# Where the independent projections stand among the attention jobs of two latent sections

## The chip, the cores and the metric

The kernel runs on one core of one Trainium2 chip. The metric is the device time of one execution in microseconds. Engines are named as in the profile: PE is TensorE (PEld is its weight load), DVE is VectorE, ACT is ScalarE, POOL is GpSimd, SP issues the DMAs.

## The reference, cut to what matters

The model is two blocks of two layers each on 256 tokens of width 1024, all in float32. The change lies in the second block alone. One of its layers computes, for the 256 latent tokens and the 256 context tokens:

```
h  = x  * (1 + scale) + shift                       # scale, shift, gate from silu(c) @ w_ada
hc = cx * (1 + scale_c) + shift_c
(a_q, a_i, a_ff, a_fb, b_q.., c_q.., d_q.., g) = split(h @ w_in)     # 1024 x 3840, the same for hc
y_a = hgrn2 scan over a_*                # forget gates, in powers of two: 1, 2, 4, ... 128 tokens
y_b = global attention (b_*)             # keys and values of latent and context tokens, normed and rotated
y_c = differential attention (c_*)
y_d = windowed attention with a sink (d_*)
y   = concat(y_a, y_b, y_c, y_d) * silu(g)
x   = layer_norm(alpha * x + gate * (y @ w_out))
```

The first layer also carries the context tokens on to the second (`cx_new`); the second layer returns the latent tokens only.

## The kernel before

The program is five sections in a row: a prologue, `one0` and `one1` (the layers of the first block), `two0` and `two1` (the latent part of the second block's layers; most of the context's work lies in `one1`). Each section has a script, a flat list of items written by `script_two0` (L338 and on) and the like. Every engine walks the same script in the same order and issues only its own part of each item. So the script fixes the order on PE, ACT, DVE and POOL at once: an instruction that waits holds up all later items on its engine.

The items that matter here:

- A **unit** is an item with 1 MB of weights of its own, streamed by SP into a ring of five slots. `("proj", name, i, (q,))` projects 256 output columns of the latent (q = 0) or context tokens (q = 1); `("out", i, (1,))` does the same for the context's output. Either is 32 matmuls, 16 for each half (L1015, L1024, L1232), into one of three PSUM banks. `("half", unit)` in a script is the first 16 matmuls, the unit's own item the other 16. ACT (L1454, L1457) or DVE (L2121) drains the bank. A unit's event e may not start before bank e - 3 is drained.
- A **job** is an attention piece over 1024 logits columns: `logits` (PE L1100), a maximum on DVE (L1872, or L1880 with a mask, then L1895), the exponentials on ACT (L1493), `soft` (DVE: L1912, L1928), `turn` (eight or four transposes on PE, L1119, copied to SBUF by ACT, L1509) and `mix` (PE L1156, copied by DVE, L1954). There is one logits buffer: `logits` of job n waits until the exponentials of job n - 1 are done (`exps_done`). `mix` of a job waits for the ACT copy of its `turn`. Each latent section has 16 jobs: 0 to 3 global (G), 4 to 7 windowed (N), 8 to 15 differential (F).
- `level` (two events, 16 matmuls, L1259, merged by DVE L2205 to L2209) and `prep` (gaps on POOL L2321 to L2327, exponentials ACT L1549, products DVE L2190 and L2192) are the steps of the scan; `hout` closes it. `decay` is DVE L2158 and L2165 with ACT L1543; `gap` is DVE L2146 and L2150.
- `sq` and `norm` are a head norm: ACT squares (L1531), PE sums (L1241), ACT L1536 and L1538, DVE L2134. `rot` is the rotary embedding: DVE L1854 and L1858, POOL L2347 and L2355. `mean` and `var` (PE L1327 to L1340) are the layer norm of the context, `feed` (DVE L2019, ACT L1588) the context's input to the second layer, and `silu`, `gate`, `mod` are elementwise.

`weave` (L133) lays a section's list `fill` of 2 x 16 slots around the jobs. Slot 2n - 1 stands beside `logits` n, behind `level` and `mix` n - 2 and ahead of `soft` n; slot 2n stands behind `turn` n - 1. So PE meets, for n from 2: `logits n, level, mix n-2, slot 2n-1, turn n-1, slot 2n, logits n+1`.

`lay(fill, start, stop, items)` fills the slots: each unit becomes two pieces, its first half and its second half, an item without weights goes with the piece before it, and the pieces are spread evenly over the slots. In `two0` 14 units go into slots 1 to 23, in `two1` 11 units into slots 0 to 18. The scan's items are placed apart by `lay_scan`, the items of later slots by hand.

Of the kernel before, what the change touches and what calls it, by code (L numbers as in the profile page):

```python
# [85 lines left out]
def jobs_latent(layer):  # L86

    out = [Job(kind, qt, [(b, 0), (b, 1)], 2 * T, 0, layer) for kind in ("G", "N") for qt in (0, 1) for b in (0, 1)]
    return out + [Job("F", qt, [(h // 2, 2 * (h % 2)), (h // 2, 2 * (h % 2) + 1)], 2 * T, 0, layer)
                  for qt in (0, 1) for h in range(4)]  # L90
# [15 lines left out]
def has_unit(item):  # L106

    return item[0] in UNIT_KINDS
# [24 lines left out]
def weave(jobs, fill):  # L133


    s = []

    def more():
        return fill.pop(0) if fill else []

    for n in range(jobs + 2):
        items = []
        if n < jobs:
            items = more()
            s.append(("logits", n))
            s += beside(items, ("level",))
        if n >= 2:
            s.append(("mix", n - 2))
        s += beside(items, ("hout",)) + [i for i in items if i[0] not in ("level", "hout")]
        if n < jobs:  # L150
            s.append(("soft", n))
        if 1 <= n <= jobs:
            s.append(("turn", n - 1))
            s += more()
    return s


def group(tag, g):

    return [("mva", 2 * g, tag), ("mva", 2 * g + 1, tag)]  # L160
# [38 lines left out]
def proj(name, q=0, i=0):  # L199

    return ("proj", name, i, (q,))
# [51 lines left out]
def latent_scan():  # L253

    out = [[("prep", 0, 0)]]
    out += [([("level", 0, LEVELS[i - 1])] if i else []) + [("prep", 0, m)] for i, m in enumerate(LEVELS[1:])]
    return out + [[("level", 0, LEVELS[-2]), ("prep", 0, "qc")], [("level", 0, LEVELS[-1])], [("hout", 0)], [("sq", "h0")],
                  [("norm", "h0")]]
# [50 lines left out]
def lay(fill, start, stop, items):  # L309


    pieces = []
    for item in items:
        if isinstance(item, list):
            pieces[-1] += item
        elif has_unit(item):
            pieces += [[("half", item)], [item]]
        else:
            pieces[-1].append(item)
    for n, piece in enumerate(pieces):  # L320
        slot = fill[start + n * (stop - start) // len(pieces)]
        if piece[0][0] == "half" or ("half", piece[0]) in slot:
            slot += piece
        else:
            slot[0:0] = piece


def lay_scan(fill, start, steps):


    for n, items in enumerate(steps):
        fill[max(start + 2 * (n - 2), 0) if n < 12 else start + n + 6] += items


def script_two0():

    out = lambda i: ("out", i, (1,))
    s = [proj("kk"), proj("vv"), ("silu", 1), ("gate", 1, 0), ("gate", 1, 1), ("rot", "nk", 0), ("sq", "gk0"), proj("gq"), ("norm", "gk0"),  # L338
         ("sq", "gq0"), proj("ff"), proj("fb"), ("rot", "gk", 0), ("gap", 0), ("norm", "gq0"), ("half", out(0)), ("rot", "gq", 0),
         ("decay", 0), out(0)]  # L340
    jobs = jobs_latent(0)
    fill = [[] for _ in range(2 * len(jobs))]
    fill[0] += [proj("hq")]
    lay_scan(fill, 3, latent_scan())
    fill[24] += [("silu", 0), ("gate", 0, 0)]
    for h, items in ((22, [("gap", 1)]), (23, [("decay", 1)]), (25, [("prep", 1, "khat")]), (27, [("khatT", 1)]), (29, [("state", 1)])):
        fill[h] += items
    lay(fill, 1, 24, [proj("nq"), out(1), ("rot", "nq", 0), out(2), out(3), proj("fk"), ("mean", 1),
                      proj("fq"), ("var", 1), ("rot", "fk", 0), ("mod", "v1"), proj("fv"), ("rot", "fq", 0), proj("hi"), ("feed", 1, "v1"), proj("ff", 1),
                      proj("fb", 1), proj("g"), proj("g", 0, 1), proj("g", 0, 2), proj("g", 0, 3)])  # L350
    lay(fill, 25, 32, [proj("hi", 1)] + [("outa", i, (0,)) for i in range(3)])
    s += weave(len(jobs), fill)
    s += [("sq", "f0"), ("half", ("outa", 3, (0,))), ("norm", "f0"), ("outa", 3, (0,)), ("gate", 0, 1), proj("vv", 1), ("outb", (0,))]
    return s + [("mean", 0), ("half", proj("kk", 1)), ("var", 0), ("feed", 0, "v1"), proj("kk", 1)]


def script_two1():

    s = [proj("kk"), ("sq", "gk1"), proj("vv"), ("norm", "gk1"), ("rot", "nk", 0), ("sq", "gk0"), proj("gq"), ("norm", "gk0"),
         ("sq", "gq0"), proj("ff"), ("affine", 0, 0), proj("fb"), ("rot", "gk", 0), ("gap", 0), ("norm", "gq0"), ("half", proj("hq")), ("rot", "gq", 0),  # L360
         ("decay", 0), proj("hq")]
    jobs = jobs_latent(1)
    fill = [[] for _ in range(2 * len(jobs))]
    lay_scan(fill, 1, latent_scan())
    fill[15] += [("silu", 0)]
    fill[20] += [("gate", 0, 0)]
    lay(fill, 0, 19, [proj("nq"), proj("g"), ("rot", "nq", 0), proj("g", 0, 1), proj("fk", 1), proj("fk"), proj("g", 0, 2), ("rot", "fk", 0),
                      proj("fq"), proj("g", 0, 3), ("rot", "fq", 0), proj("hi"), proj("fv"), proj("fv", 1)])
    for g, h in ((4, 19), (5, 21)):
        fill[h] += group("v1", g)  # L370
        fill[h + 1].append(("row", g))
    for i in range(4):
        fill[22 + i].append(("flip", i))
    lay(fill, 24, 32, [("outa", i, (0,)) for i in range(3)])
    n = next(h for h, items in enumerate(fill) if ("norm", "h0") in items)
    fill[n].remove(("norm", "h0"))
    fill[n].insert(0, ("norm", "h0"))
    s += weave(len(jobs), fill) + [("sq", "f0"), ("half", ("outa", 3, (0,))), ("norm", "f0"), ("gate", 0, 1), ("outa", 3, (0,))]
    return s + [("outb", (0,)), ("settle", 0), ("settle", 1)]
# [105 lines left out]
for _args in (("prologue", PROLOGUE, 1), ("one0", script_one0(), 1, 0, JOBS_ONE),  # L485
              ("one1", script_one1(), 1, 0, JOBS_ONE + jobs_ctx()),
              ("two0", script_two0(), 2, 0, jobs_latent(0)), ("two1", script_two1(), 2, 1, jobs_latent(1))):
    SECTIONS.append(Section(*_args, before=SECTIONS[-1] if SECTIONS else None))
# [1983 lines left out]
```

## Time and profile before

| | |
|---|---|
| Time, median of 3 runs | 1391.55 us (1390.64 to 1391.55) |
| The profiled execution | 1388.96 us, span 1387.2 us |
| PE busy | 1339.2 us (97%) |
| PEld busy | 1114.7 us (80%) |
| DVE, ACT, POOL busy | 51%, 31%, 12% |
| Mean granted TensorE clock | 0.992 of full |
| DMA | 224.89 MB, mean 162 GB/s |

Busy PE is not PE at its peak: matmuls are pipelined, and their ends are modelled. The bracket at the end of a timeline line is the idle time of the engine ahead of it, and the instruction that ended it; "xN" is how many instructions of one line and shape follow one another. In the profile `two0`'s job 0 begins at 923.3 us and `two1`'s at 1201.1 us.

### The profile page before, as it was taken

To read this page: it belongs to the slowest core of one execution; us is meant where nothing else is said; L and a number is where in the kernel's file an instruction comes from. 1 tells how busy PE (TensorE), PEld (TensorE's weight loads), DVE (VectorE), ACT (ScalarE), POOL (GpSimd) and SP (SyncE) were. 2 spreads that over 40 slices of the span, in tenths; PEclk is the share of its full clock that TensorE was granted. 3 is DMA by queue.
4 is the path that set the end of the run, shared out by engine and by line. 5 is a ranking of instruction groups with operands and counts; after the bars stand their busy time and mean duration, and the time that the engine had idled before them with its cause. 6 is when DMAs were issued, how large, how long until landed. Compare 5 with 4: busy or idle time off the path is not lost.

```text
span 1387.2 us, 18957 instructions
## 1 busy us (share of the span) xinstructions
PE 1339.2 (97%) x7394; PEld 1114.7 (80%) x7394; DVE 704.8 (51%) x1525; ACT 423.5 (31%) x776; POOL 168.2 (12%) x191
## 2 busy tenths in 40 slices
PE   6999999999899999989999999999999999999996
PEld 4888888888788888868888888887788788888864
DVE  1449677556223868414234442256674632656566
ACT  2322222311121222244323222342353513533442
POOL 0302200000020120000111100032220000323000
PEclk9999999999999999999999999999999999999999
DMA  9647557668434645534333343442222333522330
GB/s 383 271 165 285 190 192 260 222 239 316 173 127 147 242 180 185 198 119 145 129 121 122 124 143 103 148 151 92 92 91 92 116 143 122 198 92 94 111 130 31
DMA packets 31913, 224.89 MB, mean 162 GB/s; under 512 B 3920, under 2 KB 4048, under 8 KB 5072
## 3 DMA queue, kind: packets, MB, share of 16 engines
q1 hardware_dynamic: 31824, 223.68, 44.6%
q8 instruction: 59, 0.97, 0.3%
q14 instruction: 30, 0.25, 0.1%
HBM read 222.62 MB, written 1.05 MB: 161 GB/s over the span
## 4 chain that ended last, share of the span: by engine, by line
PE 87%; DVE 4%; issue 3%; DMA 2%; ACT 2%; SPq 1%; POOL 0%; DVEq 0%; ACTq 0%; POOLq 0%
PE event L1024 45%; PE event L1015 11%; PE event L1168 6%; PE event L1232 5%; PE logits L1100 4%; PE mixed_out L1156 3%; PE turns L1119 2%; DMA region<-in_quick 2%; PE event L1259 2%; PE event L1198 2%; PE event L1193 2%; PE turns L990 1%; PE logits L990 1%; PE turns L1114 1%; PE logits L1114 1%
## 5 line engine op out<-in xcount | busy, mean ns | idle before, releaser
L1024 PE MATMUL event<-u,ring 128*128 128x256 f32 x3072 | 683.7, 381 | 2.9 <-ACT u L1397 2.4
L1024 PEld LDWEIGHTS event<-u,ring 128*128 128x128 f32 x3072 | 578.6, 190 | 92.4 <-issue 15.8
L1015 PE MATMUL event<-ring,u 128*128 128x256 f32 (+1 forms) x704 | 151.1, 372 | 0.0
L1015 PEld LDWEIGHTS event<-ring,u 128*128 128x128 f32 x704 | 127.4, 190 | 18.5 <-issue 3.0
L2347 POOL TENSOR_TENSOR raw<-raw,tables 128x512 f32<-128x512 f32 (+1 forms) x28 | 44.5, 1591 | 695.0 <-DVE turned L1854 513.8
L1457 ACT ACTIVATE region<-event 128x512 f32<-128x512 f32 x72 | 43.0, 597 | 280.2 <-PE event L1024 280.0
L1493 ACT ACTIVATE S<-logits,stat 128x512 f32<-128x512 f32 (+2 forms) x160 | 83.9, 536 | 129.3 <-DVE stat L1895 124.9
L1781 DVE CUSTOM_DVE_ANT_0 region<-ring,u 128x1024 f32<-128x1024 f32 x80 | 103.8, 1298 | 2.8
L1232 PE MATMUL event<-region,ring 128*128 128x256 f32 x384 | 86.7, 385 | 2.3 <-DVE x L2121 2.3
L1168 PE MATMUL event<-region,ring 128*128 128x256 f32 x384 | 84.4, 380 | 0.1
L1232 PEld LDWEIGHTS event<-region,ring 128*128 128x128 f32 x384 | 73.5, 193 | 13.7 <-issue 3.7
L1168 PEld LDWEIGHTS event<-region,ring 128*128 128x128 f32 x384 | 72.6, 190 | 11.2 <-issue 0.9
L1100 PE MATMUL logits<-region 64*128 64x256 f32 (+4 forms) x320 | 60.9, 483 | 8.9 <-DVE region L2134 6.1
L1872 DVE TENSOR_REDUCE stat<-logits 128x2 f32<-128x1024 f32 (+1 forms) x32 | 39.2, 1224 | 59.2 <-PE logits L1100 58.7
L1509 ACT ACTIVATE PT<-turns 128x1024 f32<-128x1024 f32 (+1 forms) x52 | 44.7, 860 | 55.2 <-PE turns L1119 54.5
L1156 PE MATMUL mixed_out<-PT,region 128*64 128x128 f32 (+2 forms) x584 | 55.6, 300 | 1.7 <-ACT PT L1509 1.7
L1156 PEld LDWEIGHTS mixed_out<-PT,region 128*64 128x64 f32 x584 | 39.0, 139 | 19.0 <-issue 11.1
L2190 DVE TENSOR_TENSOR region<-region 128x512 f32<-128x512 f32 x24 | 19.1, 797 | 57.8 <-ACT region L1549 31.2
L1880 DVE CUSTOM_DVE_ANT_0 logits<-logits,tables 128x128 f32<-128x128 f32 (+2 forms) x48 | 22.9, 477 | 50.1 <-PE logits L1100 45.6
L2209 DVE COPY_PREDICATED region<-tables,event 128x512 f32<-128x512 uint32 x42 | 30.8, 734 | 34.3 <-PE event L1259 32.9
L1100 PEld LDWEIGHTS logits<-region 64*128 64x128 f32 (+1 forms) x320 | 24.8, 188 | 28.4 <-issue 23.2
L2321 POOL TENSOR_TENSOR region<-region 128x256 f32<-128x256 f32 x24 | 17.0, 708 | 248.6 <-PE event L1259 145.3
(257 smaller groups left out, 1360.9 us busy)
## 6 DMA issues: line engine op xcount, KB each, us to landing
ring<-in_w SPq DMA_DIRECT2D x196, 1024.0 KB, 4.9
region<-in_quick SPq DMA_DIRECT2D x8, 1024.0 KB, 18.2
region<-in_rows SPq DMA_DIRECT2D x1, 1536.0 KB, 8.1
tables<-in_two SPq DMA_DIRECT2D x1, 1472.0 KB, 8.0
x<-in_x SPq DMA_DIRECT2D x1, 1024.0 KB, 5.9
u<-in_cond_rows SPq DMA_DIRECT2D x1, 1024.0 KB, 7.9
x<-in_ctx SPq DMA_DIRECT2D x1, 1024.0 KB, 6.7
out<-x SPq DMA_DIRECT2D x4, 256.0 KB, 2.2
```

What stands on the lines that cost most here:

```text
L1015: ins = mm(bank[:, t * 256:t * 256 + width], mem.u[:, q, k, t * P:(t + 1) * P], wt[:, k * 256:k * 256 + width], start=k == 0, stop=k == KB ...
L1024: ins = mm(bank[:, j * 256:(j + 1) * 256], wt[:, k * 256 + j * P:k * 256 + j * P + P], mem.u[:, q, k, :], start=k == 0, stop=k == KB - 1)
L1100: ins = mm(out, q, k, start=True, stop=True)
L1156: ins = mm(out, value_of(mem, job, m, kt), turned[:, :, kt, :], start=kt == 0, stop=kt == tiles - 1)
L1168: ins = mm(bank[:, j * 256:(j + 1) * 256], wt[:, at:at + P], mem.one["y"][:, 4 * br + k, :], start=k == 0, stop=k == 3)
L1232: ins = mm(bank[:, j * 256:(j + 1) * 256], wt[:, at:at + P], src[:, k, :], start=k == 0, stop=k == KB - 1)
L1457: act(dst, split2(bank), func, scale=scale).then_inc(drained[e % BANKS], 1)
L1493: ins = act(S[:, m * K:(m + 1) * K], mem.LG[:, m * K:(m + 1) * K], ACT.Exp, bias=stat[:, 1, m:m + 1], accum_out=stat[:, 2, m:m + 1])
L1509: act(mem.PT[:, n % 2, 0:cols], mem.TR[:, 0:cols], ACT.Copy).then_inc(sems["turns_copied"], 1)
L1781: ins = eng.tensor_tensor_reduce(out=mem.scratch, in0=part, in1=times, scale=1.0, scalar=0.0, op0=ALU.mult, op1=ALU.add, accum_out=mem.mod ...
L1872: eng.tensor_reduce(stat[:, 0, 0:nm], mem.LG[:, 0:nm * K].rearrange("p (m k) -> p m k", m=nm), AX.X, ALU.max).then_inc(mine, 1)
L2347: tt(shape(mem.raw), shape(mem.raw), wide(cosine, width // T), ALU.mult).then_inc(mine, 1)
```

## The change

`lay` is replaced by `lay_whole(fill, first, last, items)` for the main filling of both sections; slots, jobs, the scan's items and everything behind job 12 are as before, and no instruction is added or dropped.

```
+def lay_whole(fill, first, last, items):
+    units = []
+    for item in items:
+        if has_unit(item):
+            units.append([item])
+        else:
+            units[-1].append(item)
+    jobs = last - first + 1
+    for k in range(jobs):
+        own = units[k * len(units) // jobs:(k + 1) * len(units) // jobs]
+        n = 2 * (first + k) - 1
+        if len(own) == 1:
+            fill[n] += [("half", own[0][0])]
+            fill[n + 1][0:0] = own[0]
+        else:
+            for i, unit in enumerate(own):
+                if 2 * i < len(own):
+                    fill[n] += unit
+                else:
+                    fill[n + 1][0:0] = unit
 ...
-    lay(fill, 1, 24, [proj("nq"), out(1), ("rot", "nq", 0), out(2), out(3), proj("fk"), ("mean", 1),
+    lay_whole(fill, 1, 11, [proj("nq"), out(1), ("rot", "nq", 0), out(2), out(3), proj("fk"), ("mean", 1),
 ...
-    lay(fill, 0, 19, [proj("nq"), proj("g"), ("rot", "nq", 0), proj("g", 0, 1), proj("fk", 1), proj("fk"), proj("g", 0, 2), ("rot", "fk", 0),
+    lay_whole(fill, 1, 9, [proj("nq"), proj("g"), ("rot", "nq", 0), proj("g", 0, 1), proj("fk", 1), proj("fk"), proj("g", 0, 2), ("rot", "fk", 0),
```

A job with one unit has its first half beside `logits` and its second behind the next `turn`; a job with two has one whole unit in each place. Read on PE, the scripts go from the left column to the right one (context units have a '; "/2" is a second half, "1/2" a first half; `level`, `mix`, `prep` are left out; "|" is the `turn`):

| `two0`, after logits | before | after |
|---|---|---|
| 1 | 1/2 nq, nq/2 \| 1/2 out1 | 1/2 nq \| nq/2 |
| 2 | out1/2, rot nq \| 1/2 out2 | 1/2 out1 \| out1/2, rot nq |
| 3 | out2/2, 1/2 out3 \| out3/2 | 1/2 out2 \| out2/2 |
| 4 | 1/2 fk \| fk/2, mean | out3 \| fk, mean |
| 5 | 1/2 fq \| fq/2, var, rot fk, mod, 1/2 fv | 1/2 fq \| fq/2, var, rot fk, mod |
| 6 | fv/2, rot fq \| 1/2 hi | 1/2 fv \| fv/2, rot fq |
| 7 | hi/2, feed \| ff' | 1/2 hi \| hi/2, feed |
| 8 | 1/2 fb' \| fb'/2 | ff' \| fb' |
| 9 | 1/2 g \| g/2 | 1/2 g \| g/2 |
| 10 | g1 \| 1/2 g2 | 1/2 g1 \| g1/2 |
| 11 | hout, g2/2, sq h \| norm h, gap', 1/2 g3 | hout, sq h, g2 \| g3, norm h, gap' |
| 12 | g3/2, decay' \| silu, gate | decay' \| silu, gate |

| `two1`, after logits | before | after |
|---|---|---|
| 0 | nq | nothing |
| 1 | 1/2 g \| g/2, rot nq | 1/2 nq \| nq/2 |
| 2 | 1/2 g1 \| g1/2 | 1/2 g \| g/2, rot nq |
| 3 | 1/2 fk' \| fk'/2, 1/2 fk | 1/2 g1 \| g1/2 |
| 4 | fk/2 \| 1/2 g2 | 1/2 fk' \| fk'/2 |
| 5 | g2/2, rot fk \| 1/2 fq | fk \| g2, rot fk |
| 6 | fq/2 \| g3, rot fq | 1/2 fq \| fq/2 |
| 7 | 1/2 hi \| hi/2 | 1/2 g3 \| g3/2, rot fq |
| 8 | silu, 1/2 fv \| fv/2 | silu, 1/2 hi \| hi/2 |
| 9 | 1/2 fv' \| fv'/2 | fv \| fv' |

## Rows read from the trace of the kernel before

**Rows 1.** The page, section 1: busy us, share of the span, instructions.

```profile
PE 1339.2 (97%) x7394; PEld 1114.7 (80%) x7394; DVE 704.8 (51%) x1525; ACT 423.5 (31%) x776; POOL 168.2 (12%) x191
```

**Rows 2.** Timeline of `two0`'s first jobs: start us, us, engine, line, operation, [idle before].

```profile
924.35 7.17 PE L1024 MATMUL event<-u,ring 128*128 128x256 f32 x32
931.46 1.13 PE L1100 MATMUL logits<-region 64*128 64x512 f32 x4
...
939.53 1.04 PE L1119 MATMUL turns<-consts,S 128*128 128x128 f32 x8
940.40 3.62 PE L1232 MATMUL event<-region,ring 128*128 128x256 f32 x16
943.95 1.13 PE L1100 MATMUL logits<-region 64*128 64x512 f32 x4
...
951.77 3.69 PE L1232 MATMUL event<-region,ring 128*128 128x256 f32 x16 [0.26 <-DVE x L2121]
...
964.18 5.38 PE L1232 MATMUL event<-region,ring 128*128 128x256 f32 x16 [2.09 <-DVE x L2121]
969.39 1.04 PE L1119 MATMUL turns<-consts,S 128*128 128x128 f32 x8
```

**Rows 3.** Windows: busy us of each engine, then granted clock, DMA share, GB/s.

```profile
964.50:967.90 3.40, 3.40 (x10) 2.68 (x9) 3.10 (x8) 0.00 (x0) 0.00 (x0) 0.50 0.54 224
602.00:609.50 7.50, 3.60 (x24) 2.84 (x24) 2.13 (x3) 2.85 (x4) 0.00 (x0) 0.55 0.16 66
```

**Rows 4.** Timeline of PE: two stalls elsewhere.

```profile
605.90 2.08 PE L1100 MATMUL logits<-region 64*128 64x256 f32 x8 [6.07 <-DVE region L2134]
...
999.57 1.10 PE L1335 MATMUL event<-u,consts 128*128 128x256 f32 x4 [2.48 <-DVE u L1363]
1000.51 3.62 PE L1015 MATMUL event<-ring,u 128*128 128x256 f32 x16
```

**Rows 5.** Timeline of `two0`, jobs 7 to 13: feed, head norm, turn.

```profile
1023.29 7.14 PE L1024 MATMUL event<-u,ring 128*128 128x256 f32 x32 [0.51 <-ACT u L1588]
...
1077.24 1.12 PE L1241 MATMUL event<-rs,consts 128*128 128x512 f32 x2 [0.97 <-ACT rs L1531]
...
1079.91 0.75 DVE L2134 SCALAR_TENSOR_TENSOR region<-region,par,rs 128x512 f32<-128x512 f32 x1 [7.46 <-ACT rs L1538]
...
1083.30 1.22 DVE L1872 TENSOR_REDUCE stat<-logits 128x2 f32<-128x1024 f32 x1
...
1086.09 0.20 ACT L1493 ACTIVATION_READ_ACCUMULATOR S<-logits,stat 128x1 f32 x1
...
1087.91 1.13 PE L1100 MATMUL logits<-region 32*128 32x512 f32 x4
1088.27 1.06 ACT L1543 ACTIVATE region<-region 128x1024 f32<-128x1024 f32 x1
1089.36 0.60 ACT L1509 ACTIVATE PT<-turns 128x512 f32<-128x512 f32 x1
...
1090.01 1.09 PE L1156 MATMUL mixed_out<-PT,region 128*64 128x128 f32 x8 [0.97 <-ACT PT L1509]
```

**Rows 6.** Timeline of `two1`'s job 0.

```profile
1201.07 1.13 PE L1100 MATMUL logits<-region 64*128 64x512 f32 x4 [0.61 <-POOL region L2355]
...
1203.84 1.23 DVE L1872 TENSOR_REDUCE stat<-logits 128x2 f32<-128x1024 f32 x1
...
1206.62 0.20 ACT L1493 ACTIVATION_READ_ACCUMULATOR S<-logits,stat 128x1 f32 x1
```

**Rows 7.** Timeline of `two1`, jobs 6 to 8.

```profile
1278.10 0.72 DVE L1854 STREAM_SHUFFLE turned<-raw 128x512 f32<-128x512 f32 x1
...
1280.75 1.26 POOL L2355 TENSOR_TENSOR region<-raw,turned 128x512 f32<-128x512 f32 x1
1281.42 1.13 PE L1100 MATMUL logits<-region 64*128 64x512 f32 x4
...
1290.23 0.88 DVE L1928 TENSOR_SCALAR S<-S,stat 128x512 f32<-128x512 f32 x2
1292.37 1.13 PE L1100 MATMUL logits<-region 32*128 32x512 f32 x4
```

**Rows 8.** The page, section 6: issues of the ring, KB each, us to landing.

```profile
ring<-in_w SPq DMA_DIRECT2D x196, 1024.0 KB, 4.9
```

## The prediction

> **What bounds the kernel now.** I read the page's busy times first: PE is busy for 1339.2 of 1387.2 us [rows 1], so it sets the end nearly everywhere, and the change adds and drops no instruction. It can act in two ways only: by PE's stalls, taken away or added, and by the clock that follows a stall. The second view is therefore the timeline of PE alone over both latent sections, where a bracket behind a row is a stall; the third is the timeline of all engines around each stall and around each place where the new order has less work on PE; the fourth, windows, for the granted clock.
>
> The reader is to see three things. First, PE's work comes in fixed bricks. A whole unit runs from 924.35 to the logits at 931.46, 7.11 us; a half from 940.40 to 943.95, 3.55 us [rows 2]. Twice a half is a whole, so cutting a unit costs nothing by itself. A job adds logits (1.0), level (1.0), mix (1.0 with sixteen matmuls) and turn (0.9): about 11 us with a unit. Second, stalls are few: 0.26, 2.09 [rows 2], 2.48 [rows 4], 0.51, 0.97 and 0.97 us [rows 5] in `two0`, and none above 0.2 us in `two1` from its first logits up to job 10. Third, behind the stall of 2.09 us the granted clock is 0.50 for 3.4 us [rows 3], its lower level, 1.2 instead of 2.4 GHz: the half that starts at 964.18 lasts until 969.39, 5.21 us in place of 3.55 [rows 2]. The stall so cost another 1.66 us behind it. Behind 6.07 us of stall in `one1` the clock is low again: 0.55 over 7.5 us, with 3.6 us of PE's work in them [rows 3, 4]. Behind 2.48 us it is not: the half at 1000.51 takes 3.62 us [rows 4]. So a stall above 2 us may bring the low clock, a long one does.
>
> **What goes.** In `two0`, `1/2 out2` and `1/2 out3` started right behind the unit before, and waited for DVE to drain a bank (0.26 and 2.09 us). Now `logits`, `level` and `mix`, 3.0 us of PE, lie between a unit and the next, more than the longer of the two waits. Gain 0.26 + 2.09 + 1.66 = 4.01 us [rows 2]. `ff'` used to begin right behind `hi/2` and waited 0.51 us for the feed; now logits, level and mix come first, while the feed keeps its distance from `hi/2`. Gain 0.51 us [rows 5]. The head norm's sum waited 0.97 us for `sq h`, with one half and a turn as cover; now g2 and g3 whole, 14 us, cover it. Gain 0.97 us [rows 5]. The wait of `mix 11` (0.97) is taken into the new sum below. The wait for `var` (2.48 us) stays: between `mean` and `var` the order is the same to the item. Sum of gains: 4.01 + 0.51 + 0.97 + 0.97 = 6.46, say 6.5 us.
>
> **What comes, A: job 12 of `two0`.** The wait for the exponentials of job 12 is the one to watch. Behind the head norm's sum stand, on DVE, the norm's product (starts 2.67 us after the sum, at 1079.91), then `gap'`, and only then the maximum of logits 12, at 1083.30; the exponentials end at 1086.29. That is 1086.29 - 1077.24 = 9.05 us from the sum, and PE's own position did not set it, since logits 12 was done before DVE came free [rows 5]. PE used to fill these 9 us with two halves of g3; both now lie ahead of the sum. Left are the sum (1.0), logits 12 (1.1), mix 10 (1.0, eight matmuls) and turn 11 (0.5): 3.6 us. Logits 13 waits 9.05 + 0.1 - 3.6 = 5.6 us. Behind it on PE are mix 11 and hi'; mix 11 also needs ACT's copy of turn 11, which stands behind the exponentials and the logarithm of `decay'`: 1.06 + 0.60 = 1.7 us [rows 5], against 1.1 us of logits 13, another 0.6 us. A = 6.2 us. Lower bound: 3.6, if `gap'` (1083.30 - 1080.66 = 2.6 us of DVE) ran ahead of the product, which DVE's order forbids; upper: 7.2, if ACT still had a drain of g3 to do in between, as it had before.
>
> **B: job 0 of `two1`.** Before, nq (7.1 us) stood between logits 0 and logits 1. Now nothing does: PE's next work needs the exponentials of job 0. DVE comes to the maximum only after the scans of `decay`, at 1203.84, and ACT ends at 1206.82 [rows 6]. Logits 0 ends its slot at 1202.1, so PE stands for 1206.82 + 0.1 - 1202.1 = 4.8 us. Queued behind logits 1 are level 0, 1/2 nq and turn 0; turn 0 then comes later than its probabilities, so no second stall. I see no bound below 4: nothing on DVE or ACT comes sooner through this change.
>
> **C: logits 8 of `two1`.** `rot fq` moves from a place ahead of logits 7 to one right ahead of logits 8, the first logits that need it. Job 7 itself keeps its order on PE (logits, level, mix, half, turn, half: 1281.42 to 1292.37). On DVE `rot` now follows soft 7, which ends at 1290.23 + 0.88 = 1291.11; the rotation takes from 1278.10 to 1282.01, 3.91 us over DVE and POOL [rows 7]. Hence 1295.0, against logits 8 at 1292.37: with 0.1 for the signal a stall of 2.7 us. Bounds: 0, if soft 7 comes 2.7 us sooner, to 5.4, twice the value, if POOL still runs gaps of the scan when the rotation reaches it. Behind logits 8 wait level, mix 6 and 1/2 hi.
>
> **The clock.** A and B are near the 6.07 us stall, so the lower level is expected behind both: 3.4 us of work at half speed, 1.7 us each; of A's, 0.5 us is work under which the 0.6 us wait of mix 11 disappears. C is near the stalls of 2.09 and 2.48 us, one with and one without: 0.6 x 1.7 = 1.0 us. Together 1.2 + 1.7 + 1.0 = 3.9 us; bounds 0 and 3 x 3.4 = 10.
>
> **What costs nothing.** Ring: the units keep their order, SP asks for the next as one ends, a load lands in 4.9 us [rows 8] while five slots hold 35 us of work; two whole units in a row do not change that. If the cover were gone, one load would cost up to 4.9. DVE in the windowed jobs: soft 7 ends 9.7 us after its logits (1281.42 to 1291.11) in a job of 10.95 us; `rot nq` and `rot fk`, 1.4 us of DVE, now stand at the end of jobs 2 and 5 with one more job before their reader. DVE's next maximum can be late by up to 1.5 us, but PE asks for its result only 11 us later. I take 0; bound 3.
>
> Cuts: in `two0` 8 units are cut by other items instead of 11, in `two1` 7 instead of 9. Rows 2 price a cut at nothing. The Trainium skill (TensorE: Matmul & The Clock Gate, "Step-by-step: what each phase is for") has PE pull a weight load ahead of running matmuls only where row groups do not conflict or a background buffer takes it; by that rule a switch between the 64-row matmuls of level and the full-height ones could leave a load in the open. At the mean load of 1114.7 / 7394 = 0.15 us [rows 1] five cuts fewer would be worth 0.8 us of gain. The row shows none of it.
>
> **Sum.** 6.2 + 4.8 + 2.7 + 3.9 - 6.5 = +11.1 us, on the profiled execution's 1388.96: 1400.1 us. The median of the runs is 2.6 us above that execution; the forecast goes on the median: 1391.55 + 11.1 = 1402.6 us.
>
> **Rivals.**
>
> 1. *Faster.* Bank turnaround is what counts. A unit that is open across `level` leaves no spare bank, and its successor waits for DVE; once cured, the pace of the whole section rises and A, B and C find DVE early. It would give at least -6.5 us, 1385 us; it decides once A + B + C with their clock stay under 6.5 us. For it: the 2.09 us row and its clock [rows 2, 3]. Against it: A and B are read off chains on DVE and ACT that do not wait for PE. The Trainium skill's rule (Trainium Kernel Development and Optimization, "Performance Expectations") that weight-load share and not matmul share tells the distance from the bound speaks for this case: 80% against 97% [rows 1]. But in an unbroken unit a matmul takes 7.11 / 32 = 0.22 us with a load beside it, so much of that room is not idle time. Chance 0.03.
> 2. *The clock stays up* behind the new stalls: +7.2 us, 1398.7. For it: the 2.48 us stall. Against it: both long ones are above 4 us. Chance 0.20.
> 3. *DVE falls behind* in jobs 3 to 7, where the rotations now come between a softmax and the next maximum: two more stalls of about 1.5 us and one more fall of the clock, +4.7 on top, 1407.3. For it: the 2.09 us stall was one by DVE [rows 2]. Against it: the credit of one job. Chance 0.17.
> 4. *Nothing to measure*: only B is real, A and C are hidden: 4.8 + 1.7 - 6.5 = 0, 1391.6. Chance 0.04.
>
> The forecast itself has 0.56. The range, 1396 to 1408, holds cases 2 and 3 with it: its low end is +4.5 us, the sum with no fall of the clock and C hidden. A measurement of this kernel tells about 0.2%, 2.8 us, from no change: slower beyond that 0.93, within it 0.04, faster beyond it 0.03.
>
> **What would show it.** A: a stall of 5 to 6 us on PE ahead of logits 13 in `two0`, ended by ACT's exponentials. B: 4 to 5 us ahead of logits 1 in `two1`, by the same. C: 2 to 3 us ahead of the first differential logits of `two1`, ended by POOL's last addition (L2355). The clock at 0.5 for some 3.4 us behind A and B. No stall by L2121 between jobs 1 and 4 of `two0`, `mean` 4 us closer to job 0, no wait at `ff'` and at the head norm. It would be wrong if logits 1 or 13 started without a wait, or if new waits for banks or for DVE's products stood between jobs 1 and 10.

## The result and the profile after

The changed kernel takes 1403.24 us (median of 4 runs, 1400.79 to 1404.21), the kernel before 1391.37: a ratio of 1.0084, 95% interval 1.0072 to 1.0096, or +11.9 us. Forecast were 1402.6 us, a range of 1396 to 1408, and 0.93 for slower.

The page after has as many instructions on every engine but for two records of ACT, a little more busy time on PE, and a longer span:

```profile
span 1402.5 us, 18955 instructions
...
PE 1345.3 (96%) x7394; PEld 1119.6 (80%) x7394; DVE 699.6 (50%) x1525; ACT 420.9 (30%) x774; POOL 166.8 (12%) x191
```

Lines of the code have moved down by 24 (L1100 is L1124). The timeline of PE after, from the first logits of `two0`, at the places that answer to [rows 2, 4, 5]:

```profile
927.27 1.13 PE L1124 MATMUL logits<-region 64*128 64x512 f32 x4 [0.62 <-POOL region L2379]
...
958.40 3.72 PE L1256 MATMUL event<-region,ring 128*128 128x256 f32 x16
961.96 1.04 PE L1143 MATMUL turns<-consts,S 128*128 128x128 f32 x8
962.84 3.62 PE L1256 MATMUL event<-region,ring 128*128 128x256 f32 x16
966.38 1.13 PE L1124 MATMUL logits<-region 64*128 64x512 f32 x4
...
969.36 7.17 PE L1256 MATMUL event<-region,ring 128*128 128x256 f32 x32
976.37 1.04 PE L1143 MATMUL turns<-consts,S 128*128 128x128 f32 x8
...
984.15 0.59 PE L1351 MATMUL event<-u,consts 128*128 128x256 f32 x2
...
999.04 1.66 PE L1359 MATMUL event<-u,consts 128*128 128x256 f32 x4 [2.48 <-DVE u L1387]
1000.63 2.08 PE L1124 MATMUL logits<-region 64*128 64x512 f32 x4
...
1083.18 1.02 PE L1265 MATMUL event<-rs,consts 128*128 128x512 f32 x2
1084.13 1.13 PE L1124 MATMUL logits<-region 32*128 32x512 f32 x4
...
1086.20 0.66 PE L1143 MATMUL turns<-consts,S 128*128 128x128 f32 x4
1092.17 2.08 PE L1124 MATMUL logits<-region 32*128 32x512 f32 x4 [5.31 <-ACT S L1517]
...
1096.08 8.32 PE L1039 MATMUL event<-ring,u 128*128 128x256 f32 x32
1104.23 0.60 PE L1143 MATMUL turns<-consts,S 128*128 128x128 f32 x4
```

The first half of the list is what was hoped for: the out units start with no bracket behind them, and from the first logits to `mean` it takes 984.15 - 927.27 = 56.9 us, where it took 61.4 (984.67 - 923.29). Then come two losses. The wait for `var` is as long as before, 2.48 us, but now the clock falls behind it: `var`'s four matmuls take until the logits 1.59 us (999.04 to 1000.63) in place of 0.94 (999.57 to 1000.51 [rows 4]), and logits 6 takes 2.08 us in place of 1.13. And logits 13 stands still for 5.31 us (A).

The timeline of all engines between the norm's sum and logits 13, against [rows 5]:

```profile
1085.75 0.75 DVE L2158 SCALAR_TENSOR_TENSOR region<-region,par,rs 128x512 f32<-128x512 f32 x1 [16.59 <-ACT rs L1562]
...
1089.12 1.22 DVE L1896 TENSOR_REDUCE stat<-logits 128x2 f32<-128x1024 f32 x1
...
1091.92 0.20 ACT L1517 ACTIVATION_READ_ACCUMULATOR S<-logits,stat 128x1 f32 x1
```

From the sum to the end of the exponentials: 1092.12 - 1083.18 = 8.94 us, against 9.05 before. The chain on DVE and ACT is unchanged; what is gone is PE's work beside it.

In `two1`, against [rows 6, 7], PE:

```profile
1207.28 1.13 PE L1124 MATMUL logits<-region 64*128 64x512 f32 x4 [0.62 <-POOL region L2379]
1213.09 2.08 PE L1124 MATMUL logits<-region 64*128 64x512 f32 x4 [4.68 <-ACT S L1517]
...
1220.88 1.04 PE L1143 MATMUL turns<-consts,S 128*128 128x128 f32 x8
...
1300.73 1.13 PE L1124 MATMUL logits<-region 32*128 32x512 f32 x4 [2.73 <-issue]
```

and DVE and POOL ahead of the last of these:

```profile
1295.80 0.88 DVE L1952 TENSOR_SCALAR S<-S,stat 128x512 f32<-128x512 f32 x2
1296.73 0.01 DVE L1878 LOAD_MASK_SELECT turned<-raw  x1
1296.73 0.72 DVE L1878 STREAM_SHUFFLE turned<-raw 128x512 f32<-128x512 f32 x1
...
1299.37 1.26 POOL L2379 TENSOR_TENSOR region<-raw,turned 128x512 f32<-128x512 f32 x1
```

B is 4.68 us, ended by ACT. C is 2.73 us; the view puts it down to "issue", but POOL's last addition of the rotation ends at 1300.63, 0.1 us before logits 8 starts. Windows behind the four stalls (granted clock is the third number from the end), answering to [rows 3]:

```profile
999.00:1003.00 4.00, 3.96 (x14) 2.20 (x16) 3.83 (x6) 0.89 (x2) 3.00 (x2) 0.57 0.46 193
1092.00:1096.00 4.00, 3.83 (x12) 2.07 (x12) 2.63 (x6) 3.91 (x6) 0.04 (x1) 0.50 0.00 0
1213.00:1216.00 3.00, 2.91 (x14) 1.88 (x16) 1.38 (x3) 1.09 (x2) 2.69 (x5) 0.50 0.00 0
1300.70:1304.00 3.30, 3.27 (x37) 2.25 (x37) 1.96 (x3) 0.49 (x1) 0.00 (x0) 1.00 0.46 191
```

The clock fell behind `var`, A and B, not behind C. At `var` it fell about half a microsecond after its first matmul had started:

```profile
999.25:999.50 0.25, 0.25 (x2) 0.22 (x2) 0.25 (x1) 0.00 (x0) 0.00 (x0) 0.89 0.93 393
999.50:999.75 0.25, 0.25 (x2) 0.17 (x2) 0.22 (x2) 0.00 (x0) 0.00 (x0) 0.50 1.08 459
```

The kernel before kept the full clock over the same stretch:

```profile
999.50:1003.50 4.00, 3.93 (x18) 3.52 (x19) 3.83 (x6) 0.89 (x2) 3.01 (x2) 1.00 0.46 193
```

The account of the two profiled executions (1388.96 and 1404.21 us, 15.2 apart): 4.0 us lie ahead of `two0`'s first logits, in code that did not change (923.29 against 927.27); over the 14 profiled executions of this document this start lies between 923.29 and 928.21 us, so the 4.0 are scatter. `two0` went from 277.8 to 280.0 us (first logits to first logits of `two1`), +2.2; `two1` from 186.1 to 195.2 us (to the end of the span), +9.1. In `two1`, from logits 0 to turn 0 after, 13.60 us hold 6.6 us of bricks, so B costs 7.0: 4.7 of stall, 2.3 of low clock. With C's 2.7 that is 9.8, less 0.7 of small waits and cuts gone. In `two0`, from the norm's sum to turn 12, 21.05 us hold 12.65 us of bricks: A costs 8.4, of which 5.3 are stall and 3.1 low clock. The low clock behind `var` adds 1.7. Against these 10.1 stand 4.5 us up to `mean`, 0.5 of the feed, 1.9 of the two waits of 0.97, and 1.0 of smaller terms, which the account of the gains below names.

### The profile page after: what moved, and what is told of

Its sections match the earlier page's. It is cut to its first block, busy times and chain, and to the rows that moved or that the text cites. A ratio compares the mean times of both kernels' runs of the same rounds, so it can differ in the third digit from the quotient of the medians.

```text
span 1402.5 us, 18955 instructions
## 1 busy us (share of the span) xinstructions
PE 1345.3 (96%) x7394; PEld 1119.6 (80%) x7394; DVE 699.6 (50%) x1525; ACT 420.9 (30%) x774; POOL 166.8 (12%) x191
## 4 chain that ended last, share of the span: by engine, by line
PE 90%; DVE 5%; issue 3%; ACT 2%; DMA 1%; POOL 0%; SPq 0%; DVEq 0%; ACTq 0%; POOLq 0%
PE event L1048 44%; PE event L1039 11%; PE event L1192 6%; PE event L1256 5%; PE logits L1124 4%; PE mixed_out L1180 3%; PE turns L1143 3%; PE event L1283 2%; PE event L1222 2%; PE event L1217 2%; PE logits L1014 1%; PE turns L1014 1%; PE event L990 1%; PE event L1027 1%; ACT S L1517 1%
## 5 line engine op out<-in xcount | busy, mean ns | idle before, releaser
L1124 PE MATMUL logits<-region 64*128 64x256 f32 (+4 forms) x320 | 63.8, 501 | 21.7 <-ACT S L1517 11.4
L1124 PEld LDWEIGHTS logits<-region 64*128 64x128 f32 (+1 forms) x320 | 25.4, 193 | 42.4 <-issue 26.2
L1180 PEld LDWEIGHTS mixed_out<-PT,region 128*64 128x64 f32 x584 | 39.7, 140 | 18.7 <-issue 11.9
L1143 PE MATMUL turns<-consts,S 128*128 128x128 f32 x336 | 45.7, 274 | 0.0
```

What stands on the lines that cost most here:

```text
L1124: ins = mm(out, q, k, start=True, stop=True)
L1143: ins = eng.transpose(mem.TR[:, i * P:(i + 1) * P], S[:, at:at + P], c["ident"])
L1180: ins = mm(out, value_of(mem, job, m, kt), turned[:, :, kt, :], start=kt == 0, stop=kt == tiles - 1)
```

## The experiments

Theory: three covers were taken from PE (A, B, C), each a stall of known length, and a low clock behind some. Rivals: whole units cost by themselves; the low clock is hidden; the stalls are only moved. Each kernel was timed in 5 rounds beside the kernel before, whose median was 1391.3 to 1391.5 us in each of the three sets. "Under" and "over" are differences of medians against the changed kernel's 1403.24 unless something else is named. A ratio's interval is about 0.1% wide on each side, 1.5 us, so a difference of two changed kernels is good to about 2 us.

**The new filling in one section alone.**

```
 t0_only: script_two1 keeps  lay(fill, 0, 19, ...)
 t1_only: script_two0 keeps  lay(fill, 1, 24, ...)
```

> The new filling in two0 alone; two1 filled as before. Theory (the three stalls A, B, C and the clock behind them): two0 carries the gains of 6.5 us and A with its clock, 7.4 to 8.5 us, so +1 to +2.5 us against the kernel before, 1392.4 to 1394; no stall ahead of logits 1 and 8 of two1. Rival (whole units cost by themselves, spread over both sections): half of the 11.9 us, about +6 us, 1397.

> The new filling in two1 alone; two0 filled as before. Theory: B 4.7 us of stall with 2.4 us of clock, C 2.7 us, clock behind C 0 to 1.7 us: +9 to +10.5 us against the kernel before, 1400.4 to 1402. Rival (spread over both sections): about +6 us, 1397.

Measured: 1395.15 us, ratio to before 1.0027 (1.0018 to 1.0037), and 1400.92, 1.0068 (1.0056 to 1.0080). `two1` carries most, +9.6, as the three stalls have it. `two0` is +3.8, above the 1 to 2.5 expected: a miss. Its ten runs lie far apart, 1392.76 to 1398.36 us. The profile of one at 1396.73 shows the expected stalls and no others, but low clock behind `var` and also behind a stall of 2.07 us late in `two1` that all kernels have, and that the change does not touch:

```profile
1336.93 1.78 PE L1200 MATMUL event<-strips,consts 128*128 128x512 f32 x2 [2.07 <-DVE strips L1793]
```

(1.78 us for what takes 1.13 in the kernel before.) The spread over both sections that the rival wanted is refused.

**One cover given back at a time.**

```
 undo_a, script_two0:
+    fill[22].remove(proj("g", 0, 3))
+    fill[23].insert(0, proj("g", 0, 3))
 undo_b, script_two1:
+    fill[0] += [proj("nq")]
-    lay_whole(fill, 1, 9, [proj("nq"), proj("g"), ...
+    lay_whole(fill, 1, 9, [proj("g"), ...
 undo_c, script_two1:
+    fill[14].remove(("rot", "fq", 0))
+    fill[12].append(("rot", "fq", 0))
```

> The changed kernel with the unit g3 of two0 moved from ahead of the head norm's sum to behind mix 10 of job 12. Theory: logits 13 finds its exponentials done; the 5.3 us of stall and about 3 us of low clock go, a wait of under 1 us for the copy of turn 11 comes back: 7 to 8 us under the changed kernel, 1395.5 to 1396.5. Rival (the changed order of the head norm or the banks, not the missing cover, is what costs): under 2 us gained, above 1401.

> The changed kernel with nq of two1 put back whole behind logits 0, the other ten units over jobs 1 to 9. Theory: the 4.7 us of stall ahead of logits 1 go and 2.4 us of low clock: 7 us under the changed kernel, 1396. If the low clock behind a stall costs nothing, since later waits take it up, 4.7 us: 1398.5. Rival (DVE's pace in jobs 1 to 4 sets the time, the stall is only moved): no gain, 1403.

> The changed kernel with rot fq of two1 moved ahead of logits 7, behind fq. Theory: the 2.7 us of stall ahead of logits 8 go, and with them what the clock cost behind it, 0 in the profiled execution: 2.7 to 4 us under the changed kernel, 1399.2 to 1400.5. Rival (the profile puts this stall down to issue, not to POOL, so the order is not what ends it): no gain, 1403.

undo_a: 1395.25 us, 8.0 under. undo_b: 1396.84, 6.4 under. Both are near what was expected. (Two of the six runs of undo_a are at 1399 to 1400 us, the others at 1395; its profile, of a run at 1398.97, has low clock behind the stall C.) The timeline of PE of undo_a at the place of A: the long bracket is gone, and the 0.97 us of [rows 5] is back.

```profile
1085.77 1.13 PE L1126 MATMUL logits<-region 32*128 32x512 f32 x4
1087.86 1.09 PE L1182 MATMUL mixed_out<-PT,region 128*64 128x128 f32 x8 [0.97 <-ACT PT L1535]
```

undo_c: 1403.05 us, 0.2 under: nothing, where 2.7 to 4 were expected. Yet the stall itself did go. The timeline of PE of undo_c at logits 8, and 45 us later at the stall of 2.07 us:

```profile
1295.43 3.62 PE L1050 MATMUL event<-u,ring 128*128 128x256 f32 x16
1298.98 1.13 PE L1126 MATMUL logits<-region 32*128 32x512 f32 x4
...
1344.31 1.16 PE L1202 MATMUL event<-strips,consts 128*128 128x512 f32 x2 [2.07 <-DVE strips L1795]
...
1346.25 2.07 PE L1126 MATMUL logits<-region 32*128 32x512 f32 x4
1348.25 1.97 PE L1182 MATMUL mixed_out<-PT,region 128*64 128x128 f32 x8
```

Logits and mix take twice their time. From that stall's end to the first `outb` matmul it is 1386.92 - 1344.31 = 42.6 us, after the change 1385.47 - 1346.07 = 39.4: 3.2 us of low clock, which paid back C. The mean granted clock that is on record for every timed run points the same way: 0.982 to 0.984 in the five runs of undo_c, 0.985 to 0.986 in the four of the changed kernel. The next experiment puts it to the test.

**The stall behind it filled.** Four matmuls that nobody reads, 1.8 us of PE, in the 2.07 us stall of the changed kernel, of undo_c and of the kernel with all three moves:

```
             elif kind == "row":
+                if item[1] == 5:
+                    eng.wait_ge(drained[e % BANKS], w.fills(e - BANKS))
+                    for _ in range(4):
+                        mm(mem.bank[e % BANKS][:, 0:256], c["ident"], mem.consts[:, 0:256], start=True, stop=True)
```

> The changed kernel with 4 filler matmuls (1.8 us of PE) in the 2.07 us stall ahead of the last mva transposes of two1 (row 5). Theory: this stall is followed by low clock in some executions and not in others, worth up to 3.2 us: 0 to 2 us under the changed kernel, 1401.2 to 1403.2.

> The kernel with rot fq moved ahead of logits 7, with the same 4 filler matmuls. Theory: the 2.7 us that this move took out of PE came back as low clock behind the later stall of 2.07 us (3.2 us in the profiled execution); with that stall filled the move shows: 2.7 to 3.2 us under the kernel without the filler, 1400, and 1.5 to 3 us under the changed kernel with the filler. Rival (the move itself gives nothing): no difference to the changed kernel with the filler.

Measured: 1402.50 and 1399.73. With the later stall filled, the move of `rot fq` is worth 2.8 us, its stall; the ranges, 1402.07 to 1403.58 and 1398.86 to 1402.24, just touch. On the changed kernel the filler does 0.7, within the uncertainty, and there the profile had shown no low clock at this place. So the 2.7 us of C are very likely real, and in undo_c they came back as low clock 45 us later.

**All three moves, without and with the filler.**

> All three moves together: g3 of two0 behind mix 10 of job 12, nq of two1 behind logits 0, rot fq ahead of logits 7. Theory: 7.5 + 7 + 2.7 = 17.2 us under the changed kernel, 1386, which is 5.4 us under the kernel before: whole units are then as good as halves or better. Rival (the gains overlap, or whole units cost by themselves): 1391 or more.

> The kernel with all three moves, with the same 4 filler matmuls. Theory: the 6.8 us of low clock that stood behind the 2.07 us stall go: 2 to 3.2 us under the three moves, 1387.2 to 1388.4. Rival: no gain, 1390.4, and the shortfall of the three moves against their sum lies elsewhere.

Measured: 1390.39 us, ratio to before 0.9982 (0.9971 to 0.9992), and 1386.16, 0.9962 (0.9949 to 0.9974). The moves alone fall 4.4 us short of the 1386 expected. Their eleven runs form two groups: five at 1386.2 to 1388.1 us with a mean granted clock of 0.989 to 0.991, six at 1390.4 to 1391.3 with 0.988. The profile is of one of the slower group (1391.25), and its windows have 0.73 and 0.50 behind the stall of 2.07 us:

```profile
1329.80:1333.00 3.20, 3.13 (x10) 1.30 (x10) 2.32 (x6) 1.72 (x4) 0.00 (x0) 0.73 1.01 422
1333.00:1336.50 3.50, 3.50 (x16) 2.76 (x15) 1.68 (x3) 1.36 (x4) 0.00 (x0) 0.50 0.28 112
```

With four useless matmuls there, the time is the expected one, and all five runs are at 1384.8 to 1386.9. The new filling with its three covers is then 5.1 us better than the old one; the kernel before was not run with the filler, but the profiles agree without it: from the first logits of `two0` to the stall of 2.07 us it is 401.87 us with the three moves (928.00 to 1329.87), 407.51 before (923.29 to 1330.80). The rival that whole units cost by themselves falls.

**The long stalls kept, PE busy in them.** In `tensor`, at the start of `logits`:

```
+                idle = {("two0", 13): 23, ("two1", 1): 20}.get((sec.name, n), 0)     # warm2: 11 and 10
+                if idle:
+                    eng.wait_ge(drained[e % BANKS], w.fills(e - BANKS))
+                for _ in range(idle):
+                    mm(mem.bank[e % BANKS][:, 0:256], c["ident"], mem.consts[:, 0:256], start=True, stop=True)
```

> The changed kernel with matmuls that nobody reads in PE's two long stalls: 23 of 128x256 ahead of logits 13 of two0, 20 ahead of logits 1 of two1, into a bank that is free. The waits stay, PE is busy in them. Theory: the granted clock stays up, and the low clock's price goes: 3.2 + 2.4 us less 0.6 us for a wait that shows again, about 5 us under the changed kernel, 1398.2; so the stalls alone cost 10 us and the clock behind them 5. Rival (the low clock is hidden, or it falls all the same): no gain or a loss, 1403 or more.

> As the kernel with filler matmuls, at the right size: a matmul in the code is two PE instructions of 0.22 us, so 11 of them (4.9 us) ahead of logits 13 of two0 and 10 (4.4 us) ahead of logits 1 of two1; the first attempt had twice as much and held PE for 10.1 and 8.9 us. Theory: the waits end when they did, the low clock behind both goes: 5 us under the changed kernel, 1398. Rival (the low clock behind these stalls is hidden by later waits): no gain, 1403.

The first, at 1405.90 us, missed by its size: one matmul of the code is two instructions on PE, and the filler outlasted the wait by some 4 us each time. The second, at the right size: 1401.01, 2.2 us under, where 5 were expected. Its timeline at A:

```profile
1085.78 4.91 PE L1076 MATMUL event<-consts 128*128 128x256 f32 x22
1091.25 1.13 PE L1129 MATMUL logits<-region 32*128 32x512 f32 x4 [0.56 <-ACT S L1522]
1092.97 1.09 PE L1185 MATMUL mixed_out<-PT,region 128*64 128x128 f32 x8 [0.59 <-ACT PT L1538]
1093.98 7.17 PE L1039 MATMUL event<-ring,u 128*128 128x256 f32 x32
```

The clock stayed up: logits 1.13 in place of 2.08 us, hi' 7.17 in place of 8.32, and the 0.6 us wait of mix 11 shows again. Logits 12 to turn 12 takes 17.8 us (1083.21 to 1101.00) against 20.1, and logits 0 to turn 0 of `two1` 11.3 against 13.6: 2.3 us each, 4.6 together. But C, untouched, is now followed by low clock:

```profile
1295.18 2.00 PE L1129 MATMUL logits<-region 32*128 32x512 f32 x4 [2.72 <-issue]
```

and from there to turn 7 it is 9.9 us (1295.18 to 1305.11) instead of 6.7. The low clock behind A and B is a price of its own, then, and not hidden in the profile; of its 4.6 us about half shows in the medians, and the 3.2 us behind C are enough for the rest. The 2.2 us are themselves little more than the uncertainty.

**The wait for `var` covered as well.** Three moves, and `two0` laid by hand over jobs 1 to 12; the core is

```
+    job(5, [proj("fq")], [("half", proj("fv")), ("var", 1), proj("fv"), ("rot", "fk", 0), ("mod", "v1")])
+    one(6, proj("hi"), ("rot", "fq", 0))
+    one(7, proj("g"), ("feed", 1, "v1"))
+    one(8, proj("ff", 1))
 ...
```

(`job` and `one` lay units as `lay_whole` does; a unit per job follows up to g3 beside logits 12.)

> The three moves, and two0 filled over jobs 1 to 12 with the first half of fv ahead of var and its second half behind it, so that PE has 3.6 us more work before it needs the sum of squares. Theory: the stall of 2.5 us ahead of var goes, and the low clock that stood behind it (1.4 us) where it fell: 2.5 to 4 us under the kernel with the three moves, 1382 to 1383.5. Rival: the same work is late elsewhere (the feed of the context's input), 1386.

1382.88 us, ratio to before 0.9930 (0.9917 to 0.9942): 8.6 us under the kernel before, 20.4 under the changed one, the best of all. `var` starts without a bracket, between the halves of fv:

```profile
996.65 3.62 PE L1055 MATMUL event<-ring,u 128*128 128x256 f32 x16
1000.11 1.03 PE L1375 MATMUL event<-u,consts 128*128 128x256 f32 x4
1000.97 3.62 PE L1055 MATMUL event<-ring,u 128*128 128x256 f32 x16
```

Against the kernel with the three moves it is 7.5 us, more than the 2.5 to 4 expected; its profile has no low clock at the 2.07 us stall either, which the other's has. Against the filled one it is 3.3. The kernel also moves the units behind fv, so the gain is not shown to be `var`'s alone.

## Why the prediction was right

**Direction and size.** +11.1 us forecast, +11.9 measured, +11.3 in the changed sections of the profiled executions. The mechanism was the predicted one at all three places, and each was tested by giving its cover back: A 8.0 us, B 6.4, C 2.8 with the later stall filled. Term by term, each stall with its clock: A 7.4 forecast and 8.4 measured, B 6.5 and 7.0, C 3.7 and 2.7, `var` 0 and 1.7, the gains 6.5 and 8.6.

**The stalls.** A was forecast at 5.6 us and is 5.31, B at 4.8 and is 4.68, C at 2.7 and is 2.73. They could be read so closely because each hangs on a chain of DVE, ACT or POOL work that keeps its length: one had to read where that chain ends and lay PE's remaining bricks beside it. The wait of mix 11 (0.6) is hidden by the low clock, as the sum allowed in part.

**The gains** were forecast at 6.5 us and are about 8.6: in `two0` 7.9, of which 4.5 up to `mean` (4.0 forecast), 0.5 and 1.9 as forecast, and 1.0 of smaller terms; in `two1` 0.7. Most of the 2.1 us more can be found in the rows. A bracket starts at the modelled end of the piece before, which is later than the time at which a piece with no wait would have been followed: `1/2 out3` started 5.81 us after `out2/2` (958.37 to 964.18), against 3.45 us from a half that has `mean` right behind it (981.22 to 984.67), so it was 2.36 us late and not 2.09, and over the five waits this makes 0.8 us. Four waits of 0.13 us, one in `two0` and three in `two1`, are gone. The cuts, below, are another 0.5.

**The clock** is the mis-sized term: 1.2 + 1.7 + 1.0 = 3.9 forecast, 3.1 + 2.3 behind A and B, 0 behind C, and 1.7 behind `var`, where I had forecast none, 7.1 in the profile. The step that failed is "The wait for `var` (2.48 us) stays": the wait did stay, but the clock behind it did not. In the 14 profiled executions the stall of 2.48 us had low clock behind it in all 11 of the new order and in neither of the 2 of the old one. The next item on PE differs too (half a unit before, logits now), but it is not shown to decide: the clock is at 0.50 by 999.50 to 999.75, and logits 6 starts at 1000.63 only. From `mean` to `var` the order on PE is the same in both kernels. What makes the difference stays open. The clock came out 3.2 us dearer than forecast, the gains 2.1 us larger and the stalls about 1 us shorter. That these cancel is luck, and it is why the sum is nearer than its terms.

**Rival 1** (faster, banks set the pace): the gain is there, but A, B and C did not find DVE early. **Rival 2** (the clock stays up) fell with the windows at 0.50. **Rival 3** (DVE falls behind in jobs 3 to 7): no new stall stands there in any profile. **Rival 4** (only B is real) fell with A and C.

**Cuts** were priced at nothing, and this reading was wrong by a little. In one stretch of the new order two halves take 3.56 and 3.54 us (958.40 to 961.96, 962.84 to 966.38), 7.10 together, and a whole unit 7.01 (969.36 to 976.37). The unit of 7.11 us in [rows 2] stands between two logits; the next unit of that trace, laid as two halves with nothing between them, takes 7.01 (932.52 to 939.53). A cut so costs 0.1 us, and five cuts fewer are worth some 0.5 us by that estimate, not nothing. The 0.8 us that was worked out beside the Trainium skill's rule on weight loads (TensorE: Matmul & The Clock Gate, "Step-by-step: what each phase is for") is of that order; that the 0.1 us is a weight load left in the open is not shown.

## What to carry to other kernels

When a script or a planner moves independent work, list for each wait of the busy engine how long its chain on the other engines is and how much work of the busy engine is left beside it; here the first job of a section and the job behind a norm needed their filler more than the other jobs needed an even spread. The rotation of an operand cost 2.7 us right ahead of its first reader and nothing a job earlier. When a small stall is removed and the time stays, look at the clock behind the later stalls, and at how the single runs are spread, before giving up the theory.

## What the runs showed of the hardware

The stalls repeat to 0.05 us from kernel to kernel; the clock behind the short ones does not. In the 14 profiled executions, low clock stood behind the stalls of 5.31 and 4.68 us each time that they occurred (6 of 6 both), behind that of 2.7 us in 3 of 7, and behind that of 2.07 us in 4 of the 11 where it was left open. The low clock takes from 1.6 to 3.2 us there, from half the stall (B) to one and a half times it (the stall of 2.07 us in undo_c). In nine kernels A, B or C was gone or filled and the stall of 2.07 us left open: in seven of them the profiled execution had low clock behind C (t1_only, undo_a, warm2) or behind the stall of 2.07 us (t0_only, undo_c, warm, the three moves), where the changed kernel had none; undo_b and the kernel with `var` covered had none either. Why it shows there rather than vanishing is open: the profile shows the level and not what sets it, and that was not tried.
